# Splitting the residual before its norm, and scaling the first linear at its read-out

## What is computed

```python
def rms_norm(x, g):
    return x * lax.rsqrt(jnp.mean(x * x, axis=-1, keepdims=True) + EPS) * g

# first block, once
proj = rms_norm(h, mix_norm_g) @ w_in            # xa, zu, zv and two gates are columns of proj
h = h + merged @ w_out                           # S5 scan, gated SGU
h = h + memory_cross_attention(rms_norm(h, xattn_norm_g), rms_norm(mem, mem_norm_g), ...)
n = rms_norm(h, ffn_norm_g); h = h + (silu(n @ w_gate) * (n @ w_up)) @ w_down
x = rms_norm(h, final_norm_g)
# second block, two layers
z = rms_norm(x, attn_norm[l]) @ w_in[l]          # four attention branches
x = x + merged @ w_out[l]
u = causal_dwconv(rms_norm(x, ffn_norm[l]) @ w_up[l], conv_w[l], conv_b[l])
x = x + (silu(a) * b) @ w_down[l]                # a, b: halves of u
return rms_norm(x, final_norm)
```

## Time and profile before

| what | value |
|---|---|
| median of 3 runs | 3268.53 us (3265.35 to 3271.07) |
| profiled execution, its own time | 3267.25 us |
| its span, first to last instruction | 3265.4 us |
| mean granted TensorE clock | 0.975 |
| PE busy | 3086.3 us, 95% |
| DVE, ACT, POOL busy | 1247.7, 1302.3, 1368.5 us |

### The profile page before, as it was taken

One profiled execution on the slowest core, in us unless ns is written; L12 is line 12 of the kernel. 1 busy time (PEld: TensorE's weight loads), 2 busy tenths in 40 slices (PEclk: granted clock), 3 DMA queues, 4 the chain that ended last, 5 costly groups with the idle time before them and its releaser, 6 DMA issues.

```text
span 3265.4 us, 47280 instructions
## 1 busy us (share of the span) xinstructions
PE 3086.3 (95%) x15373; PEld 2474.8 (76%) x15373; DVE 1247.7 (38%) x2101; ACT 1302.3 (40%) x2112; POOL 1368.5 (42%) x994
## 2 busy tenths in 40 slices
PE   5989999899998899989999999989999999999997
PEld 4768787678887676767887888877777778878886
DVE  5864221221102477654113233028575520233321
ACT  4333234333322444544323454234454432344532
POOL 3325466144443443213554555435321345535442
PEclk8999999999999999999999999999999999999999
DMA  5223334123332332212332333333221233323321
GB/s 145 75 65 123 98 103 126 38 81 96 97 96 75 86 103 82 68 36 62 97 97 81 97 96 97 97 84 107 78 66 43 66 88 97 97 80 96 97 97 59
DMA packets 214566, 283.44 MB, mean 87 GB/s; under 512 B 44322, under 2 KB 123354, under 8 KB 212698
## 3 DMA queue, kind: packets, MB, share of 16 engines
q1 hardware_dynamic: 210626, 275.62, 29.2%
q10 hardware_dynamic: 2888, 2.11, 0.3%
q0 software_dynamic: 848, 3.15, 0.3%
HBM read 265.61 MB, written 4.69 MB: 83 GB/s over the span
## 4 chain that ended last, share of the span: by engine, by line
PE 89%; DVE 6%; ACT 3%; issue 1%; POOL 0%; ACTq 0%; DVEq 0%
PE half L682 78%; PE half L1036 2%; PE half L1069 2%; PE half L1054 1%; PE half L718 1%; PE half L1126 1%; DVE rms L1823 1%; ACT arena L1214 1%; PE half L1113 1%; PE half L902 1%; PE half L818 0%; POOL wL L2530 0%; PE half L919 0%; DVE arena L2342 0%; DVE hT L1830 0%
## 5 line engine op out<-in xcount | busy, mean ns | idle before, releaser
L2530 POOL TENSOR_TENSOR wL<-slot,wH 128x512 fp32r<-128x512 f32 (+1 forms) x976 | 1344.8, 1383 | 1818.8 <-ACT wH L1223 1815.6
L1223 ACT ACTIVATE wH<-slot 128x512 fp32r<-128x512 f32 (+1 forms) x976 | 604.7, 625 | 1353.5 <-PE half L682 1353.3
L682 PE MATMUL half<-nH,wH 128*128 128x512 f32 x2336 | 932.7, 399 | 60.6 <-DVE nL L1850 38.2
L682 PE MATMUL half<-nH,wL 128*128 128x512 f32 x2336 | 919.3, 394 | 0.0
L682 PE MATMUL half<-nL,wH 128*128 128x512 f32 x2336 | 919.0, 393 | 0.0
L682 PE MATMUL half<-arena_split,wH 128*128 128x512 f32 (+1 forms) x2432 | 737.6, 386 | 9.5 <-ACT arena L1214 3.9
L682 PEld LDWEIGHTS half<-nH,wH 128*128 128x128 f32 x2336 | 444.6, 190 | 176.0 <-issue 44.9
L682 PEld LDWEIGHTS half<-arena_split,wH 128*128 128x128 f32 x2432 | 453.9, 189 | 102.5 <-issue 4.9
L682 PEld LDWEIGHTS half<-nH,wL 128*128 128x128 f32 x2336 | 444.4, 190 | 95.0
L682 PEld LDWEIGHTS half<-nL,wH 128*128 128x128 f32 x2336 | 445.2, 191 | 89.9
L682 PE MATMUL half<-arena_split,wL 128*128 128x512 f32 (+1 forms) x1216 | 467.9, 385 | 0.0
(11 more groups left out here) (290 smaller groups left out, 2467.7 us busy)
## 6 DMA issues: line engine op xcount, KB each, us to landing
slot<-in_w_in SPq DMA_DIRECT2D x344, 256.0 KB, 2.7
slot<-in_w_up SPq DMA_DIRECT2D x440, 128.0 KB, 2.1
slot<-in_w_down SPq DMA_DIRECT2D x132, 256.0 KB, 2.6
slot<-in_w_branch SPq DMA_DIRECT2D x64, 256.0 KB, 2.6
slot<-in_w_out SPq DMA_DIRECT2D x48, 256.0 KB, 2.7
slot<-in_w_gate SPq DMA_DIRECT2D x88, 128.0 KB, 2.1
arena<-arena SPq DMA_DIRECT2D x40, 256.0 KB, 4.1
slot<-in_w_proj_b SPq DMA_DIRECT2D x16, 256.0 KB, 2.8
```

The source lines that it names most:

```text
L682: mm = pe.matmul(dst, lhsT, rhs, start=(k == 0 and m == 0), stop=(k == last and m == 2))
L1223: act.activation(wH[:, p, 0:cols], slot[:, s, 0:cols], ACT.Copy).then_inc(weights_high, 1)
L2530: pool.tensor_tensor(wL[:, p, 0:cols], slot[:, s, 0:cols], plainly(wH[:, p, 0:cols]), ALU.subtract)\
```

## The change

**Split at once.** `add_first` and `add_second` replace `add_back`. While or right after a chunk is added, ACT makes `nH` = round(`hT` x gain) (`early_high`) and DVE `nL` (`early_rest`): the residual is split without its rms. The squares are now added up on DVE, so that PE needs one fp32 matmul with ones. The first linear behind the norm (`up0`, `mix1`, `xa`) multiplies these, and the sum of squares is slipped in behind its unit 4 (`at=4`). Its output is multiplied by the reciprocal root where it is read out. Meanwhile the stream is split again, normed, for the linears that follow (`split_norm` into a ring of three staging chunks; `second_linear` on ACT writes `nH[k]` once unit k of the first linear has used it).

**Exceptions.** `ss_xa` is not split early; its sum moves into `wk0`, behind unit 4, some linears ahead of `wq0`. `ss_mem` gets its squares added on DVE. At the border of the blocks the two norms become one: gains multiplied (`both`), both sums of squares formed, and `hT` itself is rescaled on DVE later, behind the selection of layer 0. For `mix`, x is loaded and turned in two halves, the S5 tables' DMAs move from SP's and ACT's queues to POOL's, the S5 input is scaled per token row, and the stream is re-split in two groups of four chunks, around `scan(1)`, from `nH`+`nL`.

**The end.** The last norm is applied per token row: `hT` x gain is turned (its first half within `dn1`), the sums are 20 matmuls with one column of ones each, and ACT scales at the read-out, with eight stores of 256 KB.

**Also.** All these hardware loops are written out straight; the NOPs and computed waits go (the top-k loops stay). In the `up` groups of the layers ACT's order changes. Transposing of a layer's vectors moves into `dn0`.

```diff
-            def add_back(jobs_of, name, l=0, next_l=0):
+            def early_rest(name, gains, k, l=0):
+                dve.wait_ge(S["early_high"], early_chunks(name, l) + k + 1)
+                dve.scalar_tensor_tensor(out=nL[:, k, :], in0=hT[:, k, :], scalar=gains[:, k:k + 1], in1=plainly(nH[:, k, :]),
+                                         op0=ALU.mult, op1=ALU.subtract).then_inc(S["early_split"], 1)
...
+            def add_second(jobs_of, name, l=0, next_l=0, gains=None):
...
+                for k in range(4, KD):
+                    dve.tensor_tensor(hT[:, k, :], hT[:, k, :], banks(h)[:, k - 4, :], ALU.add).then_inc(S["residual"], 1)
+                    if gains is not None and k > 4:
+                        early_rest(name, gains, k - 1, next_l)
...
+            def sum_rest(name, l=0):
+                dve.wait_ge(S["squared"], parts + 5)
+                add_into(S["summed_squares"], parts + 3, sq[:, 4:6, :], sq[:, 6:8, :])
+                add_into(S["summed_squares"], parts + 4, sq[:, 4, :], sq[:, 5, :])
+                add_into(S["summed_squares"], parts + 5, sq[:, 0, :], sq[:, 4, :])
...
             def split_norm(name, gains, l=0, ks=range(KD), between=None):
...
                 def whole_chunk(k):
+                    if k >= 3:
+                        dve.wait_ge(S["normed_split"], first + k - 2)
+                    if gains is None:
+                        link(dve.tensor_tensor(staged(name, k), plainly(nH[:, k, :]), plainly(nL[:, k, :]), ALU.add))
+                        dve.tensor_tensor(staged(name, k), staged(name, k), rms[:, :], ALU.mult).then_inc(S["normed_chunk"], 1)
...
+                    if between and k == 1:
+                        between()
...
-                square_sum("bss_ff", l)
-                with pe.Fori(0, 5) as i:
-                    linear("bupa", stream, l, i, ready=normed("bss_ff", l))
+                linear("bup0", stream, l, ready=unnormed("bss_ff", l), after=lambda: square_sum("bss_ff", l))
+                linear("bup1", stream, l, ready=normed("bss_ff", l))
+                for g in range(2, NG):
+                    linear(f"bup{g}", stream, l)
...
+            def second_linear(norm, first, second, l=0, cols=512):
+                round_units(second, l, 0, [0, 1], cols)
                 for k in range(KD):
+                    round_normed(norm, k, l, first)
+                    if k < 2:
+                        round_units(second, l, 0, [2 + k], cols)
+                    elif k % 2:
+                        round_units(second, l, 0, [4 + (k - 3) // 2], cols)
+                round_units(second, l, 0, [7], cols)
...
+                for g in range(NG):
+                    p = g % 2
+                    if g:
+                        ahead(f"bup{g + 1}" if g + 1 < NG else "bdn0", l)
+                    conv_last(g)
+                    if 0 < g < NG - 1:
+                        others(f"bup{g + 1}", l)
...
+                    act.wait_ge(S["taps_added"], l * NG + g + 1)
                     act.activation(conv[:, p, 0:2, :], conv[:, p, 0:2, :], ACT.Silu).then_inc(S["silu_b"], 1)
                     act.wait_ge(S["ff_ready"], l * NG + g + 1)
                     round_ff(conv[:, p, 0:2, :], g)
...
+                def scaled_up_b():
+                    done(dve, "bup0", l)
+                    dve.tensor_tensor(conv[:, 1, :, :], banks(h), all_rms(4), ALU.mult).then_inc(S["up_scaled"], 1)
...
             inputs_matrix(0)
+            dve.wait_ge(S["token_root"], 1)
+            dve.reciprocal(token_rms, token_rms).then_inc(S["token_rstd"], 1)
+            inverse_root("ass_mix")
...
             inputs_matrix(2)
+            split_norm("ass_mix", None, ks=range(4))
             scan(1)
+            split_norm("ass_mix", None, ks=range(4, KD))
```

More of the change, by code:

```diff
@@ L71 @@
          [("wo0", 8, 1), ("wo1", 8, 1)],
-         ("loop", 5, [("upa", 8, 2), ("upb", 8, 2)]), [("upc", 8, 2), ("dn0", 22, 1), ("dn1", 22, 1)]]
+         [(f"up{g}", 8, 2) for g in range(NG)] + [("dn0", 22, 1), ("dn1", 22, 1)]]
 def pad_units(parts):
@@ L887, in _ @@
             pe.wait_ge(S["mem_split"], 1)
-            for g in range(2):
-                linear(f"awk{g}", split(mH, mL), n=M)
+            linear("awk0", split(mH, mL), n=M, after=lambda: square_sum("ass_xa"))
+            linear("awk1", split(mH, mL), n=M)
             for g in range(2):
                 linear(f"awv{g}", split(mH, mL), tokens=2)
-            square_sum("ass_xa")
             for g in range(2):
@@ L953, in _ @@
                   .then_inc(S["layer_vecs_turned"], 1)
-                square_sum("bss_at", l)
-                linear("bmix1", stream, l, ready=normed("bss_at", l))
-                linear("bmix2", stream, l, tokens=NB, cols=MIX2)
+            linear("adn0", split(ffH, ffL), ready=multiplied(0), after=lambda: turn_layer_vecs(0), at=11)
+            linear("adn1", split(ffH, ffL))
+            for l in range(LAYERS):
+                linear("bmix1", stream, l, ready=unnormed("bss_at", l), after=lambda: square_sum("bss_at", l))
+                linear("bmix2", stream, l, tokens=NB, cols=MIX2, ready=normed("bss_at", l))
                 def some(name, units, tokens=None, act=stream):
@@ new lines, in _ @@
+                last = l == LAYERS - 1
+                linear("bdn0", split(ffH, ffL), l, ready=multiplied(NG + l * NG), after=None if last else lambda: turn_layer_vecs(l + 1), at=11)
+                linear("bdn1", split(ffH, ffL), l, after=(lambda: turn_out(0)) if last else None, at=15)
+            o = fill("bss_fin", 1)
+            for b in range(NB):
+                for k in (0, 4, 5, 6, 7):
+                    if k == 0:
+                        pe.wait_ge(S["summed_squares"], state_parts("bss_fin", 1) + 2)
+                    else:
+                        pe.wait_ge(S["squared"], state_parts("bss_fin", 1) + k - 2)
+                    mm = pe.matmul(o[:, b:b + 1], squares("bss_fin")[:, k, b * P:b * P + P], ones[:, 0:1],
+                                   start=(k == 0), stop=(k == KD - 1))
@@ L1188, in _ @@
+            mm.then_inc(S["summed"], 1)
+            turn_out(1)
         @block.scalar
@@ new lines, in _, with scaled_mix @@
+            add_into(S["gained_squares"], 5, gained[:, 4, :], gained[:, 6, :])
+            dve.scalar_tensor_tensor(out=gained[:, 4, :], in0=gained[:, 0, :], scalar=EPS, in1=gained[:, 4, :], op0=ALU.mult, op1=ALU.add)\
+               .then_inc(S["gained_squares"], 1)
+            dve.wait_ge(S["tables_loaded"], 16)
+            for l in range(LAYERS):
+                def scaled_mix():
+                    done(dve, "bmix1", l)
+                    h = jobs.half["bmix1"]
+                    dve.tensor_tensor(mix1, banks(h), all_rms(NB), ALU.mult).then_inc(drained[h], 1)
+                if l == 0:
+                    dve.wait_ge(S["joined_root"], 1)
+                    link(dve.reciprocal(rms[:, :], rms[:, :]))
+                    split_norm("bss_at", both, l, between=scaled_mix)
+                else:
+                    inverse_root("bss_at", l)
+                    split_norm("bss_at", vec[:, W_AT:W_AT + KD], l, between=scaled_mix)
```

816 lines of the change are left out of this document (464 added, 352 removed).

## The result

The changed kernel takes 3214.51 us (median of 4 runs, 3208.69 to 3217.68) against 3267.51 before (median of 4 as well, 3265.35 to 3271.07): ratio 0.9835, 95% interval 0.9817 to 0.9852. Faster, as forecast, but by 53 us where 84 were expected, and 2.5 us outside the range. The profiled execution is the slowest of the four: 3217.68 us, span 3215.9.

A forecast was written before the change was run, and what follows sets the result against it. PE bounds the kernel, busy 95% of the span; gains at the norms, end and straight code less the S5 loss sum to 85.1 us, taking 3267.25 to 3182.2, with the median at 3183.5; range 3155 to 3212.

The forecast's parts named there:

- rivals C and D: C: contention makes S5's additions long, 3197 to 3210, chance 0.17; D: early split doesn't carry, 3223, chance 0.09.
- D's mechanism: Stage after stage, PE waits for weights or chunks behind ACT's extra work; half the norms' 79 us lost; chance 0.09.
- The border: Between the blocks, two norms become one: 32.3 us less 4.5 of remaining costs, gain 27.8.
- PE waits some 1.2 for the second: At the border: PE's wait for the second sum of squares, with ACT's three passes a chunk and DVE's seven additions.
- a chunk's re-split with the read-out in front of it: 0.9: In `mix2` at the border: units of 204 columns are about half as long as a chunk's re-split, costing 0.9 us.
- The S5 stage: First stage: 4 us earlier start against 10.4 us of uncovered re-split, loss 6.4 us, bounds 0 and 20.
- I count 4 us earlier: S5 stage: from DVE's first taps matrix on, 4 us earlier; bounds 10 earlier and 4 later.
- `ss_at` 1: Second layer's attention norm: costs of 0.9, 0.5 and 0.5 against 17.9 us, gain 16.0.
- `ss_ff` in the layers: Layers' feed-forward norms: 13.8 us less 0.9 and 5.7 for a hole before `up2`, gain 7.2 twice, 14.4.
- the common part: At each early-split norm: PE pays one matmul, 0.93 us, and no slow start, instead of 13.8 us.
- The end: Behind `dn1`'s last unit: 19 us to the end instead of 27.7, gain 8.7, bounds 5 and 13.
- 20 small fp32 matmuls with a column: Sums of the last norm at the end: taken as 5 us, bounds 1 and 9.

The follow-up runs named there:

- ACT's new order: The changed kernel with ACT rounding one weight of `mix2` behind each of the first six re-split chunks instead of every second one: 3202.72 us, ratio 0.9803.
- experiment 2: The changed kernel with ACT rounding the first three weights of `up2` before the silu of group 0 in both layers: 3197.30 us, ratio 0.9786.
- five edits: The changed kernel with `up2`'s and `mix2`'s weights sooner, border additions per chunk, S5 re-split of chunks 4 to 7 later, x-attention roundings before `xv`'s read-out: 3176.05 us.
- the run before it: The changed kernel with ACT rounding the x-attention's first two re-split chunks before `xv`'s second read-out, but behind `wq0`'s first weights: 3208.23 us, ratio 0.9819.

## Why the prediction was wrong

**Right in kind.** The waits for `nL` went where they should, the first linears run unnormed without a stop before unit 4, the reciprocals lie beside matmuls, a hole ended by `POOL wL` stands before `up2` in both layers, and a hole of 12.1 us before the third taps (about 12 forecast). `ss_mem` with `ss_xa`, and the first block's `ss_ff`, came within 1.5 us. The result lies between rivals C and D. D's mechanism ("PE waits for weights or chunks") is what `mix2` showed, and I gave it 0.09; it is not there "in stage after stage", and it isn't the larger part.

**Mis-sized, in the order of size** (the table's differences, 35.6 us in all, of which 3 come from the profiled execution being the slowest of its four):

- *The border* lacks 10.3. Two steps failed. "PE waits some 1.2 for the second" sum: it waited 0.98 and 3.19, the second sum took 2.1 us instead of 0.9, and half of unit 5 ran at the lower clock. I had counted DVE's "seven additions" at the lengths they have alone; six of them took 9.36 us, four of these beside POOL, where 5.2 would stand alone. With the additions spread, 8 to 10 us of it came back. And for `mix2`, "a chunk's re-split with the read-out in front of it: 0.9" asked only when chunks are there, not when ACT gets to the weights: three waits, 3.7 us, and one unit at the lower clock. ACT's new order brought back 4 to 6. The two overlap: with both, the border took no less than with the additions alone.
- *The S5 stage* lacks 9.7, and the re-split has next to no part in it. The step that failed is "I count 4 us earlier", in two parts. The first taps came at 89.85 instead of 90.75, 0.9 earlier, and 0.0 to 2.4 earlier in nine other profiles with the same start. I had left out that ACT's first work would wait for vectors crowded by loads that the change itself had moved forward: with the weights behind the vectors the taps came 4.6 to 5.5 earlier. The second part I had at nothing: from the first taps to the wait behind the second taps it took 25.1 us before, without a wait for DVE at the first taps and at a granted clock of 1.00. Afterwards it took 28.0 in twelve profiles and 32.3 in three, the changed kernel's own among them, with waits of 2 to 4 us for DVE at the first taps, 1.5 to 4.8 at the turning behind them, and a clock of 0.84 to 0.95. In the three, that second wait is 4.84 and the clock of the stretch 0.84.
- *`ss_at` 1* lacks 5.1: `mix2`'s weights again, 3.7 of it measured.
- *`ss_ff` in the layers* lacks 4.0, and the hole isn't where. It was forecast as a wait of 3.6 us and took 4.8, since I had left the table load of 1.28 us before the silu out of ACT's chain; but with the slow start it had been priced at 5.7, and removing it brought 6.0 and 5.8. Without the hole the layers gain 10.5 and 11.7 and the first block 11.4, where 13.8 less 0.9 was forecast. So the common part, a norm's 13.8 us against one matmul, is 1.2 to 2.4 too high each time. 0.5 us of it is a wait for the third re-split chunk; the rest stays open.
- *The end* lacks 3.7: 20.6 us from the last unit to the end of the span, where I had 17. The term is that of the "20 small fp32 matmuls with a column", which I took at 5 us: they took 8.69, all at 0.21 us a record (two to a matmul) and a granted clock of 0.53. With the edit of experiment 2 they took 6.86, 18 of the 40 at 0.11, and the end was 1.9 us shorter.

So most of the norms' gain was there, and part of the rest was held by the order of the work around it: five edits that only move instructions, four of which did anything, brought back 38 us, the re-split and the holes, which the forecast had counted as losses, among them.

**The contention** was my rival C, and placed wrong. In the re-split of the S5 stage, where I had looked for it, DVE's instructions kept the short kind (0.68 and 0.69 us, with the last pairs at 1.47 for two), because POOL idled 12.5 and 14.6 us around the two halves: what I had noted against C. It bit at the border instead: 0.69 us alone, 1.67 beside POOL, and in the first matrices of the S5 stage (last section). The Trainium skill ("SBUF — State Buffer", Who interferes with whom) says that a DVE instruction with two inputs in SBUF contends with a GpSimd instruction that reads SBUF; the rows at 532.94 to 540.40 agree, 1.78 beside POOL and 0.74 or 0.68 alone.

## What to carry to other kernels

When work is moved under the cover of another stage, write down for that stage what each helper engine issues and in which order, the next linear's weights first: the waits in `mix2` and before `up2` sat in ACT's program order, those at the border's sums and the third taps in DVE's, and each place cost a few moved lines. Where two helpers slow each other, count the durations beside the other, and start chains of small additions as their inputs come. A wait that comes back in another place can still be the cheaper one, if the feeders get ahead while the engine stands. And compare several profiles of the same code before a stage's time is laid to an edit.

## What the runs showed of the hardware that was not expected

- DVE and POOL alternate: beside POOL's rests, DVE's 128x512 instructions started exactly 1.70 us apart (532.94, 534.64, 536.34, 538.04), while POOL took 9.36 us for six instead of 7.79 in the run before it. Alone, a DVE instruction takes 0.68 to 0.75 and POOL's 1.29.
- Small loads issued by 9.3 us landed at 20.0 to 21.7 with 256 KB weight loads and small-row tables in flight, and at 13.2 or 14.05 with either of them held back.
- A DVE TENSOR_SCALAR of 64x64 fp32 took 2.91 to 5.02 us instead of 0.19 when it fell into POOL's issuing of tables and its two clearings, in four profiles, and ended within 0.1 us of the second clearing.
- The same code took 172.9 to 175.2 us around the border in different runs, and from the first to behind the second taps either 28.0 or 32.3, nothing between. The forms go with where DVE's products of 1152 elements meet POOL's rests. In the slower form (all three profiles) the last product of the first taps' matrix is of the short kind, 1.35 us, and two of the six for the next matrix are long, 2.43 and 2.41; PE gets its first taps sooner and then waits 4.84 us for the turning. In the other form (five profiles read) the last product is mostly the long one, 2.41, the next six are all short, 1.34, and PE waits 1.5 to 3.0. What tips it was not tried.
